# Four weight chunks of the second layer kept in gather slots between its two tiles

## The reference

```
h = rms_norm(x, norm1_g);  proj = h @ w_in        # q, k, v (512 each), f_logit (8), u_pool (256), u_ssm (256)
att  = forgetting_attention(q, k, v, f_logit + f_bias, q_gain, k_gain)     # 8 heads x 64, causal
pool = multiscale_pool(u_pool, pool_w, pool_scale)                         # trailing windows 2, 4, 8, 16
ssm  = s5_mixer(u_ssm, ...)                                                # complex scan over time, GLU
x = x + concat(rms_norm(att), rms_norm(pool), rms_norm(ssm)) @ w_out

h = rms_norm(x, norm2_g);  q = h @ w_q            # 8 heads, two halves of 128
scores = q . sub_keys;  top 16 of each half, then top 16 of the 256 sums -> experts, gates
x = x + sum over the 128 picked experts of  gate * gelu(h . u_tab[e]) * v_tab[e]
```

## Time and profile before

| | us |
|---|---|
| median of 3 runs | 1538.98 |
| lowest, highest | 1538.16, 1539.54 |
| profiled execution, its own time | 1538.02 |
| its span, first to last instruction | 1536.2 |

### The profile page before, as it was taken

One profiled execution on the slowest core, in us unless ns is written; L12 is line 12 of the kernel. 1 busy time (PEld: TensorE's weight loads), 2 busy tenths in 40 slices (PEclk: granted clock), 3 DMA queues, 4 the chain that ended last, 5 costly groups with the idle time before them and its releaser, 6 DMA issues. The chain is left out here.

```text
span 1536.2 us, 19450 instructions
## 1 busy us (share of the span) xinstructions
PE 1053.8 (69%) x6790; PEld 529.0 (34%) x6790; DVE 1083.7 (71%) x2530; ACT 575.6 (37%) x1769; POOL 585.4 (38%) x526
## 2 busy tenths in 40 slices
PE   8998557868665766678766566788677645565565
PEld 6685213325332333332433234343353311111111
DVE  8768997677978776564688858565588984454454
ACT  5644424614434442452334431354343432221222
POOL 0034344443333333343433433434334345454441
PEclk9999767898878878788888788879898877768867
DMA  9289999999999999999999999999999999999995
GB/s 385 88 336 421 421 421 421 420 422 421 421 419 422 421 417 416 422 420 422 421 421 420 414 421 412 420 413 419 422 420 421 421 421 421 422 422 421 421 421 246
DMA packets 86353, 621.19 MB, mean 404 GB/s; under 512 B 9968, under 2 KB 10096, under 8 KB 11760
## 3 DMA queue, kind: packets, MB, share of 16 engines
q0 software_dynamic: 73728, 536.90, 84.2%
q1 hardware_dynamic: 12528, 83.05, 13.2%
HBM read 618.87 MB, written 1.05 MB: 404 GB/s over the span
## 5 line engine op out<-in xcount | busy, mean ns | idle before, releaser
L630 POOL DMA_INDIRECT slots<-experts,idx x512 | 581.9, 1136 | 909.0 <-PE psum L1875 739.8
L1475 DVE CUSTOM_DVE_ANT_0 slots<-slots,h 128x1024 f32<-128x1024 f32 x512 | 615.4, 1225 | 371.4 <-DMA slots<-experts,idx 367.3
L1875 PE MATMUL psum<-slots,diag 64*64 64x512 f32 x4088 | 608.3, 746 | 341.3 <-ACT diag L987 341.2
L1875 PEld LDWEIGHTS psum<-slots,diag 64*64 64x64 f32 x4088 | 177.9, 167 | 721.9 <-ACT diag L987 419.8
L971 ACT ACTIVATE ge<-ge 128x4 f32<-128x4 f32 x130 | 26.7, 205 | 472.1 <-DVE ge L1475 471.2
L971 ACT ACT_TABLE_LOAD x55 | 70.6, 1283 | 220.9 <-DVE ge L1475 220.6
L987 ACT ACTIVATE diag<-cst,ge 128x64 f32<-128x64 f32 x511 | 136.6, 336 | 6.3 <-PE psum L1875 2.0
L978 ACT ACTIVATE ge<-ge,gate 128x1 f32<-128x1 f32 x512 | 109.1, 283 | 4.2
L1798 PE MATMUL psum<-work,ring 128*128 128x128 f32 x512 | 63.3, 285 | 7.6 <-DMA ring<-weights 7.6
L1798 PE MATMUL psum<-hT,ring 128*128 128x128 f32 x480 | 59.7, 286 | 9.8 <-DMA ring<-weights 8.9
L1798 PEld LDWEIGHTS psum<-work,ring 128*128 128x128 f32 x512 | 61.7, 201 | 8.2 <-issue 8.2
(11 more groups left out here) (297 smaller groups left out, 1119.7 us busy)
## 6 DMA issues: line engine op xcount, KB each, us to landing
ring<-weights SPq DMA_DIRECT2D x30, 1152.0 KB, 9.8
ring<-weights SPq DMA_DIRECT2D x26, 1024.0 KB, 9.4
slots<-weights SPq DMA_DIRECT2D x11, 1024.0 KB, 21.5
slots<-experts,idx POOLq DMA_INDIRECT x512, 21.9
ring<-weights SPq DMA_DIRECT2D x2, 1056.0 KB, 9.5
sml<-small SPq DMA_DIRECT2D x2, 652.0 KB, 14.2
slots<-weights SPq DMA_DIRECT2D x1, 1056.0 KB, 8.8
xs<-x SPq DMA_DIRECT2D x2, 512.0 KB, 13.7
```

Of the source, the lines that this page charges most:

```text
L630: pool.indirect_dma_start(out=slot[:, place(E), :], out_offset=None, in_=src, in_offset=bass.IndirectOffsetOnAxis(ap=idx[:, n % 2, e:e + 1 ...
L1475: ins = dve.tensor_tensor_reduce(u, u, h2[:, n % 2, :], 1.0, 0.0, ALU.mult, ALU.add, d[:, i:i + 1])
L1875: ins = pe.matmul(acc[HALF * half:HALF * half + HALF, i, :], diag[rows, d % DIAGS, :], slot[rows, place(E), D + half * 512:D + half * 512 ...
```

## The change

For tile steps 2 and 3, four chunks (u, qkv0, qkv1, qkv2) are no longer loaded through the ring but once, for step 2, into four of the gather slots, and stay there until step 3 has used them. Meanwhile the gathers go round the slots that are left. `tenants()` works out which gather takes which slot. It walks through the 512 gathers with a queue of free slots; at gathers 145, 157, 161 and 165 the slot next in turn is taken out for a chunk, and at gathers 280, 292, 296 and 300 it is put back, at the head. From 165 to 279 nine slots are in use and gather E waits for expert E - 9; at the edges the distance is 12, 11 or 10. Gathers 280, 292, 296 and 300 wait instead for the chunk's use by step 3.

SyncE issues the four loads in its stream of ring loads: u's ahead of the ring load of step 2's p, the three others ahead of that of step 2's qkv3. Each first waits for the expert that was in the slot: 132, 145, 150 and 155. The ring list then has 50 loads, and load c still waits for the use of load c - 2.

```
+KEEP = {CH_SSM: "u", CH_Q: "qkv0", CH_Q + 1: "qkv1", CH_Q + 2: "qkv2"}
+
+def group_of(n, i):
+    at = ORDER.index(("mix", KEEP[i], n))
+    return next((b, q) for kind, b, q in reversed(ORDER[:at]) if kind == "open")
+
 def in_slot(n, i):
-    return (n == 0 and i < CH_ROUTE) or (n == 1 and i < CH_OUT)
+    return (n == 0 and i < CH_ROUTE) or (n == 1 and i < CH_OUT) or (n >= TILES and i in KEEP)
...
+def tenants():
+    free, last, turns = collections.deque(PLACES), {}, collections.Counter()
+    taken, back = {}, {}
+    for i in KEEP:
+        n, quad = group_of(TILES, i)
+        taken[PICKS * n + GRP * (quad - 4) + SLOTS] = i
+        n, quad = group_of(TILES + 1, i)
+        back[PICKS * n + GRP * quad + 8] = i
+    picks, kept = [], {}
+    for E in range(PICKS * STEPS):
+        if E in taken:
+            at = free.popleft()
+            kept[taken[E]] = (at, last[at])
+        if E in back:
+            at = kept[back[E]][0]
+            free.appendleft(at)
+            last[at] = -1 - back[E]
+        at = free.popleft()
+        turns[at] += 1
+        picks.append((at, last.get(at), turns[at]))
+        last[at] = E
+        free.append(at)
+    return picks, kept
+
+TENANTS, KEPT = tenants()
 def place(E):
-    return PLACES[E % SLOTS]
+    return TENANTS[E][0]
...
@@ block.sync, ahead of each ring load
+                for k in KEPT:
+                    if (n, i) == next(u for u in USES[uses(TILES, k):] if u in RING):
+                        at, before = KEPT[k]
+                        sp.wait_ge(S["expert_done"], by_tensor(before + 1))
+                        sp.dma_start(slot[:, at, 0:width(k)], weights[1, k, :, 0:width(k)]).then_inc(kept_in[k], 16)
...
@@ block.gpsimd, gather()
+                    elif TENANTS[E][1] < 0:
+                        pool.wait_ge(S["chunk_used"], uses(TILES + 1, -1 - TENANTS[E][1]))
                     else:
-                        pool.wait_ge(S["expert_done"], by_tensor(E - SLOTS + 1))
+                        pool.wait_ge(S["expert_done"], by_tensor(TENANTS[E][1] + 1))
...
@@ block.vector, dots()
-                    dve.wait_ge(landed[place(E)], 16 * (E // SLOTS + 1))
+                    dve.wait_ge(landed[place(E)], 16 * TENANTS[E][2])
...
@@ block.tensor, chunk()
+                if in_slot(n, i) and n >= TILES:
+                    pe.wait_ge(kept_in[i], 16)
+                    at = KEPT[i][0] * 2 * D
+                    return slots[:, at:at + width(i)]
```

More of the change, by code:

```diff
@@ L10 @@
+import collections
 from contextlib import ExitStack
@@ L458, in trunk @@
         chunk_in = [sem(f"chunk_in{i}") for i in range(CH_ROUTE)]
+        kept_in = {i: sem(f"kept_in{i}") for i in KEPT}
         landed = [sem(f"slot_in{i}") for i in range(SLOTS)]
```

## The result

The changed kernel took 1553.91 us in the median of four runs (1552.52 to 1555.60), the kernel before 1538.57 (1538.14 to 1539.54). The ratio is 1.0101, with a 95% interval of 1.0088 to 1.0113, so 15.3 us slower. The forecast was 1542 with a range of 1531 to 1551. The profiled execution is the slowest of its four, 1555.6 us with a span of 1553.8; against the one before its span is longer by 17.6 us.

What follows compares the result with a forecast made beforehand. The prediction took the 16 DMA engines, at about 421 GB/s, as the limit: -10.0 for removed loads, +12.9 idle DMA, +1 delayed scan, sum +3.9, rounded down to +3.5, gave 1542 us, range 1531 to 1551.

Steps and rivals of the forecast that it cites:

- The saving: Four loads of 1.049 MB fewer for tile step 3, all where DMA is the limit: 10.0 us go.
- The 1 for the scan: Step 2's chunk loads, issued earlier, delay gathers 160 to 163 and so VectorE's dots and scan: 1 us charged.
- full at gather 165: Early chunk loads keep the queue full until about 572 us, so gather 165, landing at 570.0, is not late.
- rival 3: A kept chunk comes late for TensorE because SyncE waits for the expert in its slot: 1547 us; chance 0.03.
- 177: Gather 177 waits for expert 168 and lands at 608.2, before at 602.9; DMA idle 3.2 us.
- 193 to 213: Gathers 193, 201 and 209 late by 0.6, 1.6 and 1.7, sum 3.9 us; 197, 205 and 213 in time or within the shift.
- 265: Gather 265 waits for expert 256 and lands at 860.7 against 858.8: 1.9 us of idle DMA.
- 277: Gather 277 lands at 893.6 against 892.3, since the chunk load that lay here is gone: 1.4 us.
- 290: Gather 290 lands at 932.0 against 929.5, the chunk loads that filled the hole being removed: 2.5 us.
- Rival 1: Slots become the bound, about 1 us more in each turn of nine gathers: 1548 to 1555 us; chance 0.20.
- The upper bound of 7.8 us: Gather latency behind a nearly empty queue at most 7.8 us: each place costs 2 us more, about +15, 1553.
- The average: Nine slots turn over in 22.4 us; less an average hold of 10.5, 11.9 us remain, so nine are enough on average.

Runs made afterwards that it cites:

- e2: Kernel before with 13 slots, but tile step 3 computes qkv0, qkv1 and qkv2 with u's chunk, leaving out three loads: 1532.49 us, ratio 0.996.
- the first two rows of the table: The changed kernel with only one chunk kept (u, 12 slots) or two (u and qkv0, 11 slots): 1536.05 and 1533.69 us, ratios 0.9987 and 0.9974.
- e1: The changed kernel without its kept chunks: the same slots withheld, all 58 ring loads of the kernel before stay: 1562.98 us, ratio 1.0164.
- e6: Kernel before, all loads, with four slots withheld from gather 145 to 217 only (mixer rows of step 1): 1553.87 us, ratio 1.01.
- e7: Kernel before, all loads, with four slots withheld from gather 217 to 264 only (the routing rows): 1539.69 us, ratio 1.0009.
- e4: The changed kernel with only u and qkv0 kept: 11 slots from gather 157 to 279, two loads fewer: 1533.69 us, ratio 0.9974.
- the control with all slots: Kernel before, 13 slots, all loads, with TensorE adding the waiting group of experts before a row's mixer work, not after: 1538.85 us, ratio 1.0001.

## Why the prediction was wrong

Slower was the side that had the larger chance, and the sum named the right cause, DMA that stands idle. Its size was off: +3 was forecast and +15 measured.

- **The saving held.** 54 loads, 616.99 MB, 10 us by the bytes; e2 and the first two rows of the table agree.
- **The loads moved early cost nothing, as the sum had it but for 1 us.** The 1 for the scan was not paid, and the queue was not full at gather 165 as the text says. Still, e1 loses 4.3 us there and the changed kernel none. TensorE had its kept chunks in time (it waited 0.5 us in all for loads into slots); rival 3 is out.
- **The places held in the main.** 177, 193 to 213, 265, 277 and 290 are where the gathers fall back, and nothing is lost between 223 and 264 or behind 295. e6 and e7 say the same of the part up to 264. Within the row of 193 to 213 two places were wrong: 201, given 1.6, cost nothing, and 197 and 205, said to come out in time, cost 2.6 and 3.0 with the gather behind each.
- **The failed step is the price of each place**, the sum 3.2 + 3.9 + 1.9 + 1.4 + 2.5 = 12.9, with 1 for the scan. From the table, less the 1.1 us that the run was late before:

| stretch | summed | measured |
|---|---|---|
| to gather 193 | 4.8 | 7.1 |
| 193 to 223 | 3.3 | 7.4 |
| 223 to 276 | 1.9 | 2.7 |
| 276 to 280, with one load gone | 1.4 | 2.5 + 2.5 = 5.0 |
| 280 to 295, with three loads gone | 2.5 | -3.1 + 7.5 = 4.4 |
| all | 13.9 | 26.6 |

26.6 less 10.0 and with the 1.1 is the 17.7 of gather 295. The sum was half of the cost. The largest single term was gather 177: by gather 185 (637.97 against 630.22) the run was 7.8 us late, so 177 had cost 6.7 and not 3.2.

The latency of a gather that finds the queue empty was not the error. Gather 290 alone:

```profile
DMA to landing us min/median/max: 5.4/5.4/5.4
```

Gather 193, issued at 652.61, was used at 658.31, 5.7 us later. (Gather 177 took 7.4, from 604.23 to 611.58, as the ring load issued at 602.94 went ahead of it.) What I left out is what stands around a first gather. The trace shows the three effects below; how much of the 13 us each is worth was not measured apart.
- The idle time begins before the last landing. At 600 us I let it begin when gather 176 lands. The DMA line falls to 2 tenths at 598.5, 3 us before VectorE's dot of that gather at 601.66, and to 0 right after. A landing is the last of 16 completions. From 599 to 601 the rate is 16 to 33 GB/s, about what one engine of 16 moves (421 / 16 = 26), so the others are idle by then.
- The gathers behind the first are late again. 194 came 3.1 us behind 193, and not 2.49, and from 193 to 202 the shift grew by 3.0, most of it at 197 and 198, where I had 1.6 at 201. I saw the 3.4 in the earlier trace rows, priced it at up to 2 us, and took none of it.
- I let a shift apply to both sides and drop out. It need not be the same on both. Before the burst at 907.73, gather 276 was 18.3 us late, but gather 266, on which VectorE had waited 5.2 us, had been 20.9 late: the chunk load issued at 873.24 landed ahead of gather 267, where its counterpart (859.78) had landed behind it. That exchange is 2.5 us without idle DMA, and gather 271 landed only 18.4 late, but its dot was 20.4 late (897.60 against 877.20). So the release came later against the landings than in the kernel before: 907.73 - 887.83 = 19.9. Gather 277 landed at about 907.73 + 5.7 = 913.4, against 908.08 + 2.49 = 910.6, so a hole of 1.4 became 2.8 before its second gather was counted.

Rival 1 had the right price (1548 to 1555), with the wrong picture: it wanted a loss in every turn of nine, also in the routing rows, and e7 shows none clear of noise. The upper bound of 7.8 us for a gather, given as +15 and 1553, was the nearest figure in the text; it stood for "each place costs 2 us more", which is about what happened. That is luck as far as the reason goes: it had the 2 us from a latency of 7.8, and the first gathers at 193, 277 and 290 took 5.4 to 5.7. I priced each place by its first gather alone. The average, 11.9 us left for a gather that needs 5.8, was sound and e7 bears it out; it says nothing on the mixer rows.

By the Trainium skill (DMA: Bandwidth & Descriptors, section Anatomy of one DMA) the latency was 4.4 us as an estimate, and the sum a gain of 5; the 5.4 and 5.7 us measured here are above it. What the Trainium skill says of repeating gaps as a sign of too few buffers (Perfetto Trace Analysis, section Optimization Strategy) fits the dips in the rate, with the addition that here they follow the hold and not the count.

## What to carry to other kernels

A ring of buffers in front of a saturated queue has slack only as long as something is in flight at the thinnest moment: read the number in flight just before each late release, and leave at least two of the smallest of them. Below that, price the whole burst and not its first transfer. Here four gathers were in flight at 602.45 in the kernel before, and of the slots taken two were free (-4.6 us for two chunks kept, e4), the third cost all that three chunks save, and the fourth cost 17.7 us for 2.5.

An earlier release is not free either. Adding first brought back 12 us with nine slots, but it puts a wait in front of the mixer work, and the control with all slots is where that shows.

## What the runs showed of the hardware that was not expected

The 16 completions of one gather are spread out, and the more the deeper the queue. In the kernel before, those of gather 176, issued 25.1 us before it landed, came from 592.5 to 600.4 us, 8 us apart; in the changed kernel, issued 9.8 us before and with the queue running dry behind it, from 598.6 to 601.5. So a landing time overstates how full the queue is: the rate was 98 GB/s and less for the 3 us before that gather counted as landed.
